# Three passes for all K-tiles of gate and up, and the low parts of the down weights all on GpSimd

## The chip, the cores and the metric

The kernel runs on one core of a Trainium2 chip. The metric is the device time of one execution, in microseconds. The engines are TensorE (PE in the profile; PEld is its weight load), VectorE (DVE), ScalarE (ACT), GpSimd (POOL) and SyncE (SP), which issues most DMAs.

## The reference

Two layers work on 512 tokens of width 1024, all in float32. Each layer is a mixer (three kinds of attention, gates, output projection) and then a mixture of 16 experts:

```python
h = rms_norm(x, norm_mix_g[l]);  x = x + hybrid_mixer(h, ...)
h = rms_norm(x, norm_ffn_g[l]);  x = x + hier_moe(h, ...)
# hier_moe: every token picks one group of four, and two experts in it
hid = silu(h @ w_g[e]) * (h @ w_u[e])     # w_g, w_u: 1024 x 256 for each expert
hid = hid * gate[e]                       # 0 for tokens that did not pick e
y   = sum over e of hid @ w_d[e]          # w_d: 256 x 1024
```

## The kernel before

A float32 matrix product is made in one of two ways. Native: one matmul on the float32 operands, which the trace shows as two records. Three passes (`three`, L895 to L897): each operand is split into a high part in the type fp32r and a low part, the difference, and three matmuls add high times low, low times high and high times high.

The mixer's dense products are all in three passes: GpSimd makes the high part (L763) and the low part (L769) of the streamed weights. After the mixer the rows are normalized, the router picks, and every expert gets up to 128 tokens, whose rows GpSimd gathers from DRAM (L807). A last loop takes experts with more tokens (one such block in this input).

The experts are counted from 0 in the order of work. For each of them TensorE makes, in this order: gate and up together (`gate_up`, eight K-tiles of 128x512, gate in the left half), the transposes of the next expert's gathered rows (`turn_gathered`, L1152), the down product of the expert before (`down`, two halves c of 512 columns) and the two transposes of its own hidden rows (`turn_hidden`, L1210). Experts 0 and 1 are native in gate and up. From 2 to 15, K-tiles 0 to 3 are native (L1200) and K-tiles 4 to 7 are in three passes. The down product is in three passes but for expert 15.

The other engines' orders in step e of the expert loop are written out by hand:

- ScalarE: silu(e); the first half of the transposed rows of e+1, four copies with the norm's gain as scale (L1565), and the high part of the second half (L1576); the result rows of e-1, first half (L1602); the high parts of the down weights of e, two of 1024 columns (`weights_hi`, L1593, each waits until the down product of e-1 has used its half); the high parts of K-tiles 4 to 7 of e+2 with the gain as scale (`gate_up_hi`, L1583).
- VectorE: hidden product of e (L2206); low part of the second half of the rows of e+1 (L2171); result rows of e-1, second half (L2216); high and low part of the hidden rows (L2226, L2228); the low part of half c = 1 of the down weights (`down_lo_half`, L2192); the low parts of K-tiles 4 to 7 of e+2, 512 columns each (`gate_up_lo`, L2184). Steps 0 to 3 also hold small operations of the routing.
- GpSimd: the gather for e+3 (L807); the low part of half c = 0 of the down weights, two subtractions of 512 columns (`weights_lo`, L831); the scattered addition of the result rows of e-1 to the residual in DRAM (L821).

TensorE's `gate_up(e)` waits for VectorE's and ScalarE's parts of the rows of e, and each three-pass K-tile for its low part.

The weights of an expert come in three pieces of 1 MB: K-tiles 0 to 3 of gate and up, K-tiles 4 to 7, and down. They pass through a ring of six slots in `work`, in the order `PIECE_ORDER`, issued by SyncE (L686 to L693), each after a wait for the slot's last user. Gate and up rows are 1 KB long in DRAM, and each goes to its own partition; down rows are 4 KB long.

## Time and profile before

| | us |
|---|---|
| median of 3 runs | 1399.3 (1398.26 to 1400.98) |
| the profiled execution | 1398.75 |
| its span, first to last instruction | 1396.8 |
| TensorE busy | 1363.1 (98%) |
| VectorE busy | 863.2 (62%) |
| GpSimd busy | 728.4 (52%) |
| ScalarE busy | 585.8 (42%) |

The expert stage of the first layer lies from about 520 to 690 us, that of the second from about 1209 to the end. The rest is the mixer. Matmuls overlap in the pipeline, so that the time from one start to the next is what one costs, not its duration. In a timeline neighbours of one kind are merged into one row with their count.

### The profile page before, as it was taken

What the parts mean: (1) busy time and instruction counts of PE and PEld (TensorE: products, weight loads), DVE (VectorE), ACT (ScalarE), POOL (GpSimd) and SP (SyncE); (2) the same over time, 40 slices, a digit from 0 to 9 for tenths busy, and PEclk for the clock granted to TensorE, in tenths of its full rate; (3) what the DMA queues carried; (4) which work ended last, traced back from release to release, by engine and by line L of the source; (5) the groups of instructions that cost most, each with busy time, mean ns of one, the idle gap of its engine ahead of it and who ended that gap; (6) DMA issues with size and microseconds to landing.
All of it is one profiled execution on the core that took longest, in us unless ns stands there. A gap on an engine that the chain in (4) does not pass through costs nothing.

```text
span 1396.8 us, 19901 instructions
## 1 busy us (share of the span) xinstructions
PE 1363.1 (98%) x6916; PEld 1036.2 (74%) x6916; DVE 863.2 (62%) x2057; ACT 585.8 (42%) x1334; POOL 728.4 (52%) x587
## 2 busy tenths in 40 slices
PE   7999999999999999999889999999999999999997
PEld 5788877777777876767477888777777778667674
DVE  4487866656684347776346787666567741576772
ACT  4323333343433135676443432433434421466761
POOL 4566645445345634566555576454444455255663
PEclk9999999999999999999889999999999999999999
DMA  5436422222212659999732242222222128599995
GB/s 154 130 100 172 121 83 73 73 74 97 90 61 76 232 217 318 340 360 350 190 118 76 61 135 81 75 76 74 89 80 90 61 88 292 213 330 350 346 348 130
DMA packets 148570, 224.28 MB, mean 161 GB/s; under 512 B 18635, under 2 KB 95877, under 8 KB 148463
## 3 DMA queue, kind: packets, MB, share of 16 engines
q1 hardware_dynamic: 136030, 197.59, 43.6%
q0 software_dynamic: 9936, 16.81, 5.1%
q10 hardware_dynamic: 2496, 8.52, 1.6%
q8 instruction: 59, 0.97, 0.3%
q14 instruction: 49, 0.39, 0.1%
HBM read 215.47 MB, written 31.25 MB: 177 GB/s over the span
## 4 chain that ended last, share of the span: by engine, by line
PE 92%; DVE 4%; ACT 1%; POOL 1%; DMA 1%; issue 1%; SPq 0%; POOLq 0%; ACTq 0%; DVEq 0%
PE bank L895 22%; PE bank L897 21%; PE bank L896 21%; PE bank L1200 9%; PE bank L1071 4%; PE bank L1083 3%; PE bank L1104 2%; PE bank L1152 2%; PE bank L1024 1%; PE bank L1094 1%; DVE probs L1913 1%; PE bank L1037 1%; POOL w_lo L769 1%; PE bank L1162 1%; PE bank L1360 0%
## 5 line engine op out<-in xcount | busy, mean ns | idle before, releaser
L769 POOL TENSOR_TENSOR w_lo<-raw,w_hi 128x512 fp32r<-128x512 f32 (+2 forms) x288 | 359.2, 1268 | 16.4 <-ACT w_hi L1641 4.6
L763 POOL TENSOR_SCALAR w_hi<-raw 128x1024 fp32r<-128x1024 f32 (+2 forms) x142 | 149.4, 1052 | 417.3 <-PE bank L897 414.5
L896 PE MATMUL bank<-w_hi,hT_lo 128*128 128x512 f32 (+2 forms) x696 | 258.8, 372 | 0.0
L895 PE MATMUL bank<-w_lo,hT_hi 128*128 128x512 f32 (+2 forms) x576 | 216.8, 376 | 2.1 <-DVE hT_lo L1738 1.2
L897 PE MATMUL bank<-w_hi,hT_hi 128*128 128x512 f32 (+2 forms) x576 | 211.8, 368 | 0.0
L895 PE MATMUL bank<-hT_lo,w_hi 128*128 128x512 f32 x384 | 159.5, 415 | 0.0
L897 PE MATMUL bank<-hT_hi,w_hi 128*128 128x512 f32 x384 | 150.7, 393 | 0.0
L896 PE MATMUL bank<-hT_hi,w_lo 128*128 128x512 f32 x384 | 150.2, 391 | 0.0
L896 PEld LDWEIGHTS bank<-w_hi,hT_lo 128*128 128x128 f32 x696 | 131.6, 189 | 20.3
L1200 PE MATMUL bank<-work,ptmp 128*128 128x512 f32 x288 | 129.4, 593 | 1.0 <-ACT ptmp L1565 1.0
L895 PEld LDWEIGHTS bank<-w_lo,hT_hi 128*128 128x128 f32 x576 | 108.7, 189 | 28.0 <-issue 8.7
L831 POOL TENSOR_TENSOR w_lo<-work,w_hi 128x512 fp32r<-128x512 f32 x64 | 105.7, 1672 | 43.8 <-ACT w_hi L1593 43.8
L897 PEld LDWEIGHTS bank<-w_hi,hT_hi 128*128 128x128 f32 x576 | 108.7, 189 | 17.9
L895 PEld LDWEIGHTS bank<-hT_lo,w_hi 128*128 128x128 f32 x384 | 72.1, 188 | 32.8 <-issue 20.5
L1200 PEld LDWEIGHTS bank<-work,ptmp 128*128 128x128 f32 x288 | 52.0, 190 | 54.0 <-issue 52.6
L807 POOL DMA_INDIRECT probs<-normed_dram,slot_token x32 | 33.3, 1040 | 102.5 <-PE bank L1152 80.4
L897 PEld LDWEIGHTS bank<-hT_hi,w_hi 128*128 128x128 f32 x384 | 72.1, 188 | 16.5
L896 PEld LDWEIGHTS bank<-hT_hi,w_lo 128*128 128x128 f32 x384 | 72.3, 188 | 12.5
L895 PE MATMUL bank<-oT_lo,w_hi 128*128 128x512 f32 x192 | 79.4, 413 | 0.5 <-DVE hT_lo L1971 0.5
L897 PE MATMUL bank<-oT_hi,w_hi 128*128 128x512 f32 x192 | 76.0, 396 | 0.0
L896 PE MATMUL bank<-oT_hi,w_lo 128*128 128x512 f32 x192 | 75.7, 394 | 0.0
L1496 ACT ACTIVATE probs<-probs,job_neg 128x256 f32<-128x256 f32 (+5 forms) x128 | 66.5, 523 | 15.4 <-DVE job_neg L1896 15.4
(331 smaller groups left out, 2651.4 us busy)
## 6 DMA issues: line engine op xcount, KB each, us to landing
work<-in_w_ff_gate SPq DMA_DIRECT2D x66, 512.0 KB
work<-in_w_ff_up SPq DMA_DIRECT2D x66, 512.0 KB
work<-in_w_ff_down SPq DMA_DIRECT2D x33, 1024.0 KB
raw<-in_w_gate SPq DMA_DIRECT2D x48, 512.0 KB, 3.8
raw<-in_w_in SPq DMA_DIRECT2D x40, 512.0 KB, 3.6
raw<-in_w_branch SPq DMA_DIRECT2D x24, 512.0 KB, 3.6
raw<-in_w_out SPq DMA_DIRECT2D x16, 512.0 KB, 3.9
normed_dram<-mixed ACTq DMA_DIRECT2D x8, 512.0 KB, 2.7
```

Source lines behind the costliest of these rows:

```text
L763: nc.gpsimd.tensor_scalar(w_hi[:, two, :, 0:w], raw[:, slot, :, 0:w], 1.0, 0.0, ALU.mult, ALU.add).then_inc(split_hi, 1)
L769: last = nc.gpsimd.tensor_tensor(w_lo[:, two, kk, 0:w], raw[:, slot, kk, 0:w], w_hi[:, two, kk, 0:w].bitcast(F32), ALU.subtract)
L807: nc.gpsimd.indirect_dma_start(out=gather_rows[:, e % 2, :], out_offset=None, in_=xn_dram, in_offset=bass.IndirectOffsetOnAxis(ap=rows, ax ...
L831: last = nc.gpsimd.tensor_tensor(w_lo[:, c, f, :], rows[:, f, c * 512:(c + 1) * 512], w_hi[:, c, f, :].bitcast(F32), ALU.subtract)
L895: nc.tensor.matmul(out_ap, s_hi, m_lo, start=start, stop=False)
L896: nc.tensor.matmul(out_ap, s_lo, m_hi, start=False, stop=False)
L897: return nc.tensor.matmul(out_ap, s_hi, m_hi, start=False, stop=stop)
L1071: last = nc.tensor.matmul(S[m][:, cols], q[r, job.u, job.i * P:(job.i + 1) * P], k[r, keys], start=True, stop=True)
L1083: last = nc.tensor.transpose(T[0][:, col:col + P], prob_bufs[job.g % 3][:, mm, b * P:(b + 1) * P], ident[:, :])
L1104: last = nc.tensor.matmul(O[HD * m:HD * (m + 1), job.i * P:(job.i + 1) * P], v, p[:, m, b * P:(b + 1) * P], start=(b == 0), stop=(b == len ...
L1200: last = nc.tensor.matmul(G[e % 2][:, :], et[:, e % 2, kt * P:(kt + 1) * P], gate_up_piece(n % RING)[:, :, kk, :], start=(kt == 0), stop=( ...
L1496: last = nc.scalar.activation(p, p, ACT.Exp, bias=job_neg[:, g % 4, m:m + 1], scale=-1.0, accum_out=job_sum[:, g % 4, m:m + 1])
```

## The change

All eight K-tiles of gate and up of experts 2 to 15 go through three passes (`SPLIT_FROM = 0`). ScalarE makes their high parts in four operations of two K-tiles (1024 columns), VectorE their low parts likewise, four of 1024 columns, which are written over the raw weights in their slot; so the slot is free only when TensorE has used it. VectorE also makes the low part of the first half of the gathered rows. VectorE's half of the down weights' low parts moves to GpSimd, which makes all four subtractions of 512 columns, over the raw weights too.

The ring gets nine slots, three for each kind of piece: six in `work`, two in `X`, one in the buffer `w_lo`. The order of loads changes, and the pieces of expert 2 no longer wait for expert 0. Gate and up rows are moved two at a time, in runs of 2 KB, so that a partition holds neighbouring rows; the columns of the normalized rows are put in the same order.

The norm's gain is no longer a scale of ScalarE's and VectorE's copies: GpSimd multiplies it into the rows ahead of the routing, eight operations of 512 columns, seven of them before it takes the inverse root and one after; ScalarE then scales these rows by the root. Copies of transposed rows are single operations without scale.

```diff
-RING = 6
+SLOTS_OF_PART = ((0, 3, 6), (1, 4, 7), (2, 5, 8))
+AHEAD = 3
+
+ROW_RUN = 2
...
-FIRST_SPLIT = 2
-
-PIECE_ORDER = [(2, 0), (2, 1), (2, 2), (3, 0), (3, 1), (4, 1)]
-for before in range(2, N_EXPERTS - 1):
-    PIECE_ORDER += [(e, part) for e, part in ((before + 2, 0), (before + 1, 2), (before + 3, 1)) if e < N_EXPERTS]
...
+FIRST_SPLIT, SPLIT_FROM = 2, 0
+SPLIT_PAIRS = (8 - SPLIT_FROM) // 2
+
+PIECE_ORDER = [(2, 2), (2, 0), (2, 1), (3, 0), (3, 1)]
+for e in range(4, N_EXPERTS):
+    PIECE_ORDER += [(e, 0), (e, 1), (e - 1, 2)]
+PIECE_ORDER.append((N_EXPERTS - 1, 2))
...
                 def load_piece(e, part):
-                    n = PIECES * e + part
-                    slot, old = n % RING, e - 2
+                    old = e - AHEAD
                     if old >= 0 and part == 0:
                         sp.wait_ge(first_half, old + 1)
-                    elif old >= 0 and part == 1 and splits(old):
-                        sp.wait_ge(gu_lo, split_count(old))
                     elif old >= 0 and part == 1:
                         sp.wait_ge(gu_done, old + 1)
                     elif old >= 0:
-                        sp.wait_ge(down_lo, old + 2)
-                        if old:
-                            sp.wait_ge(down_lo_dve, old)
+                        sp.wait_ge(down_done, 2 * (old + 1))
...
+                def gain_step(t, c):
+                    pool.wait_ge(g_free, 4 * (OUT_CHUNK + c) + t + 1)
+                    cols = slice(c * 512, (c + 1) * 512)
+                    in_order = lambda rows: rows.rearrange("p (a n k) -> p a k n", n=P, k=ROW_RUN)
+                    nc.gpsimd.tensor_tensor(xn[:, t, cols].rearrange("p (a k n) -> p a k n", n=P, k=ROW_RUN),
+                                            in_order(X[:, t, cols]), in_order(ffn_gain[:, cols]),
+                                            ALU.mult).then_inc(x_gained, 1)
+
+                pool.wait_ge(gain_in, 32)
+                for t in range(TT):
+                    gain_step(t, 0)
+                for t in range(TT - 1):
+                    gain_step(t, 1)
                 pool.wait_ge(ms_done, TT + 1)
                 pow_step(row_rs[:, 1, :], row_ms[:, 1, :], TT).then_inc(rs_done, 1)
+                gain_step(TT - 1, 1)
...
                 def weights_lo(e):
                     rows = down_rows(e)
-                    for c in range(1 if e else 2):
+                    for c in range(2):
                         pool.wait_ge(down_hi, 2 * e + c + 1)
                         for f in range(2):
-                            last = nc.gpsimd.tensor_tensor(w_lo[:, c, f, :], rows[:, f, c * 512:(c + 1) * 512],
+                            last = nc.gpsimd.tensor_tensor(down_low(e)[:, f, c * 512:(c + 1) * 512],
+                                                           rows[:, f, c * 512:(c + 1) * 512],
                                                            w_hi[:, c, f, :].bitcast(F32), ALU.subtract)
                         last.then_inc(down_lo, 1)
...
+                        if kt == SPLIT_FROM:
+                            pe.wait_ge(et_dve, e + 1)
+                        if (kt - SPLIT_FROM) % 2 == 0:
+                            pe.wait_ge(gu_lo, split_pairs(e - 1) + pair + 1)
+                        last = three(G[e % 2][:, :], et_hi[:, e % 2, rows], et_lo[:, e % 2, rows],
+                                     pair_hi_of(e, kt)[:, (kt - SPLIT_FROM) % 2, :], gate_up_low(e, part)[:, :, kk, :],
+                                     kt == 0, kt == KT - 1)
...
             def gate_up_hi(e):
 
-                n = PIECES * e + 1
-                act.wait_ge(piece_in[n % RING], 32 * (n // RING + 1))
-                for kk in range(4):
-                    nc.scalar.activation(gu_hi_bufs[e % 2][kk].rearrange("p (h n) -> p h n", h=2),
-                                         gate_up_piece(n % RING)[:, :, kk, :], ACT.Copy,
-                                         scale=pcol[:, ROW_FFN + 4 + kk:ROW_FFN + 5 + kk]).then_inc(gu_hi, 1)
+                for part, kk, kt in split_tiles():
+                    if kt == SPLIT_FROM or kk == 0:
+                        act.wait_ge(arrived(e, part), loaded(e, part))
+                    nc.scalar.activation(pair_hi_of(e, kt).rearrange("p k (h n) -> p k h n", h=2),
+                                         gate_up_piece(e, part)[:, :, kk:kk + 2, :].rearrange("p h k n -> p k h n"),
+                                         ACT.Copy).then_inc(gu_hi, 1)
...
             def gate_up_lo(e):
 
-                n = PIECES * e + 1
-                for kk in range(4):
-                    v.wait_ge(gu_hi, split_count(e - 1) + kk + 1)
-                    nc.vector.scalar_tensor_tensor(gu_lo_bufs[e % 2][kk].rearrange("p (h n) -> p h n", h=2),
-                                                   gate_up_piece(n % RING)[:, :, kk, :], pcol[:, ROW_FFN + 4 + kk:ROW_FFN + 5 + kk],
-                                                   gu_hi_bufs[e % 2][kk].bitcast(F32).rearrange("p (h n) -> p h n", h=2),
-                                                   ALU.mult, ALU.subtract).then_inc(gu_lo, 1)
-
-            def down_lo_half(e):
-
-                v.wait_ge(down_hi, 2 * e + 2)
-                nc.vector.tensor_tensor(w_lo[:, 1, :, :], down_rows(e)[:, :, 512:1024], w_hi[:, 1, :, :].bitcast(F32),
-                                        ALU.subtract).then_inc(down_lo_dve, 1)
+                for n, (part, kk, kt) in enumerate(split_tiles()):
+                    v.wait_ge(gu_hi, split_pairs(e - 1) + n + 1)
+                    nc.vector.tensor_tensor(gate_up_low(e, part)[:, :, kk:kk + 2, :].rearrange("p h k n -> p k h n"),
+                                            gate_up_piece(e, part)[:, :, kk:kk + 2, :].rearrange("p h k n -> p k h n"),
+                                            pair_hi_of(e, kt).bitcast(F32).rearrange("p k (h n) -> p k h n", h=2),
+                                            ALU.subtract).then_inc(gu_lo, 1)
```

## Rows read from the trace of the kernel before

**Rows 1.** The page: busy time and the chain that ended last; TensorE's native group.

```profile
PE 1363.1 (98%) x6916; PEld 1036.2 (74%) x6916; DVE 863.2 (62%) x2057; ACT 585.8 (42%) x1334; POOL 728.4 (52%) x587
...
PE 92%; DVE 4%; ACT 1%; POOL 1%; DMA 1%; issue 1%; SPq 0%; POOLq 0%; ACTq 0%; DVEq 0%
...
L1200 PE MATMUL bank<-work,ptmp 128*128 128x512 f32 x288 | 129.4, 593 | 1.0 <-ACT ptmp L1565 1.0
```

**Rows 2.** Timeline of TensorE: start us, us, engine, line, what, count.

```profile
542.07 1.45 PE L1200 MATMUL bank<-work,ptmp 128*128 128x512 f32 x3
...
604.21 3.60 PE L1200 MATMUL bank<-work,ptmp 128*128 128x512 f32 x8
...
608.34 0.40 PE L895 MATMUL bank<-oT_lo,hT_hi 128*128 128x512 f32 x1
...
610.44 1.04 PE L1152 MATMUL bank<-ident,probs 128*128 128x128 f32 x8
...
614.28 3.60 PE L1200 MATMUL bank<-work,ptmp 128*128 128x512 f32 x8
...
674.66 2.74 PE L1200 MATMUL bank<-work,ptmp 128*128 128x512 f32 x6
```

**Rows 3.** Timeline of VectorE in the same period (in brackets: idle before it, releaser).

```profile
600.98 0.42 DVE L2206 TENSOR_TENSOR sq<-sq,bank 128x256 f32<-128x256 f32 x1 [0.46 <-ACT sq L1685]
602.76 0.69 DVE L2171 TENSOR_TENSOR hT_hi<-bank,hT_hi 128x512 fp32r<-128x512 f32 x1 [1.36 <-ACT hT_hi L1576]
604.19 0.75 DVE L2216 TENSOR_SCALAR mixed<-bank,slot_weight 128x512 f32<-128x512 f32 x1 [0.74 <-PE bank L897]
...
605.65 1.25 DVE L2192 TENSOR_TENSOR w_lo<-work,w_hi 128x1024 fp32r<-128x1024 f32 x1
606.83 1.76 DVE L2184 SCALAR_TENSOR_TENSOR hT_hi<-work,pcol,hT_lo 128x512 fp32r<-128x512 f32 x1
```

**Rows 4.** Timeline of ScalarE in the same period.

```profile
601.00 1.14 ACT L1565 ACTIVATE ptmp<-bank,pcol 128x128 f32<-128x128 f32 x4
602.02 0.62 ACT L1576 ACTIVATE hT_hi<-bank 128x512 fp32r<-128x512 f32 x1
...
603.42 1.99 ACT L1593 ACTIVATE w_hi<-work 128x1024 fp32r<-128x1024 f32 x2
605.31 2.55 ACT L1583 ACTIVATE hT_lo<-work,pcol 128x512 fp32r<-128x512 f32 x4
```

**Rows 5.** Timeline of GpSimd in the same period.

```profile
602.17 1.03 POOL L807 DMA_INDIRECT probs<-normed_dram,slot_token  x1 [2.17 <-PE bank L1152]
604.55 3.49 POOL L831 TENSOR_TENSOR w_lo<-work,w_hi 128x512 fp32r<-128x512 f32 x2 [1.34 <-ACT w_hi L1593]
...
605.79 2.25 POOL L831 TENSOR_TENSOR w_lo<-work,w_hi 128x512 fp32r<-128x512 f32 x1
...
608.20 1.86 POOL L821 DMA_INDIRECT residual_dram<-mixed,slot_token  x1 [0.15 <-issue]
```

**Rows 6.** Windows: busy us (instructions) of each engine, PEclk, DMA share, GB/s.

```profile
549.00:569.00 20.00, 20.00 (x86) 13.93 (x85) 17.70 (x34) 14.02 (x26) 12.80 (x8) 1.00 1.03 340
...
599.00:649.00 50.00, 50.00 (x210) 34.91 (x209) 37.03 (x51) 35.22 (x65) 31.62 (x21) 1.00 1.06 354
...
606.00:608.00 2.00, 2.00 (x7) 1.00 (x6) 2.00 (x2) 1.86 (x4) 2.00 (x1) 1.00 1.03 409
```

**Rows 7.** Timeline of VectorE in the first experts.

```profile
544.66 1.24 DVE L2128 TENSOR_SCALAR raw<-rank 128x8 f32<-128x8 f32 x1
...
547.32 1.42 DVE L2184 SCALAR_TENSOR_TENSOR hT_hi<-work,pcol,hT_lo 128x512 fp32r<-128x512 f32 x2
```

**Rows 8.** Timelines of GpSimd and VectorE ahead of the routing.

```profile
493.59 1.29 POOL L769 TENSOR_TENSOR w_lo<-raw,w_hi 128x512 fp32r<-128x512 f32 x1
...
504.92 1.02 POOL L751 TENSOR_TENSOR row_rs<-row_ms,half_neg 128x4 f32<-128x4 f32 x1 [10.04 <-DVE row_ms L1773]
...
509.04 0.24 DVE L2016 TENSOR_TENSOR score<-bank,row_rs 128x80 f32<-128x80 f32 x1 [0.71 <-PE bank L1282]
```

**Rows 9.** DMA in the stretch from 549 to 665 us.

```profile
DMA packets 29117, 40.39 MB, mean 348 GB/s; under 512 B 2681, under 2 KB 24807, under 8 KB 29110
...
q1 hardware_dynamic: 25806, 34.19, 84.5%
```

229 lines of the change are left out of this document (129 added, 100 removed).

## The prediction

> **What bounds the kernel now.** I read the page first, busy shares and the chain that ended last [rows 1]. TensorE is busy 98% of the span and holds 92% of the chain. Every microsecond that the expert stage takes from TensorE shortens the kernel, as long as the other engines keep pace. So the question is who comes next when TensorE gets shorter.
>
> Then one period of the expert stage on TensorE [rows 2]. Expert 8's native K-tiles begin at 604.21 us and expert 9's at 614.28 (experts are counted from 0, as in the code): a period of 10.07 us. Four native K-tiles are eight records in 3.60 us, the last of them 0.59 long [rows 1]: (3.60 - 0.59)/7 = 0.43 us from one to the next, 0.86 for a K-tile. Of the three-pass matmuls nine lie between 608.34 and the transposes at 610.44, 0.233 us each, so 0.70 for a K-tile. The part outside gate/up (transposes, down product, turning of the hidden rows) runs from 610.44 to 614.28: 3.84 us.
>
> Then the same period on the other three engines [rows 3 to 5], and the stage by windows [rows 6]. VectorE is busy 7.4 of 10 us (8.85 in the experts that also carry routing work), ScalarE 7.0, GpSimd 6.3, DMA more than full at about 350 GB/s.
>
> What decides is inside [rows 3, 5]. GpSimd's low part of 128x512 takes 1.27 to 1.29 us alone [rows 5, 8] (3.49 for two, of which the second starts 1.24 after the first), and 2.25 when it is issued at 605.79, behind VectorE's subtraction of 605.65 to 606.90: it ends 1.14 us after that one. VectorE's next operation of 512 columns, 0.74 where nothing interferes (two in 1.42 [rows 7]), takes 1.76: it ends 0.55 us after GpSimd's. Even an operation on eight columns took 1.24 us beside such a pair [rows 7]. Operations of VectorE that read two operands from SBUF and GpSimd's subtractions take turns. Those with one operand in a bank (0.69 to 0.75 us) show no such stretch.
>
> **The change, part by part.**
>
> *TensorE.* Four K-tiles go from 0.86 to 0.70 us. With the first three-pass matmul after a native one, which comes later by 0.4 than its fellows, the trace has 6.23 us for the eight (604.21 to 610.44) and the change 24 x 0.233 = 5.58: 0.65 us less per expert, in 14 experts and two layers 18.2 us less. A TensorE-bound period would be 24 x 0.233 + 3.84 = 9.42 us.
>
> *ScalarE.* The four copies of 1.14 us with a scale become one copy of 0.62; four high parts of 512 columns (2.55) become four of 1024, by [rows 4] 0.97 apart, 3.9. It would end them 8.9 us after gate/up ended: still inside 9.42. Not the limit.
>
> *VectorE.* Per expert one more low part of the gathered rows (0.61 apart), and the low parts of the weights, 1.18 + 4 x 0.66 us before, become four of 1024 columns at 1.18, the step from 605.65 to the next operation: 4.72 [rows 3]. Unhindered, from the end of one expert's low parts to the start of the next ones: hidden product 0.40, two low parts of gathered rows 1.22 (durations of 0.42 and 0.69 less the overlap with the next), then from the row at 604.19 to the one at 605.65 (result rows, hidden rows high and low) 1.46, together 3.08. With 4.72 that is 7.80.
>
> *GpSimd.* Four subtractions per expert for two. It starts them when ScalarE's first high part of the down weights is there, at 604.55, or 4.18 us after gate/up ended (one period before 610.44, at 600.37).
>
> *The two together.* VectorE runs: 3.08 us, then its four, in turn with what GpSimd still has. In turn, GpSimd's costs 1.14 (above) and VectorE's of 1024 columns 0.55 x 2 = 1.10. Let T be the period and count from the end of VectorE's low parts. TensorE's next gate/up waits for the low parts of its rows, 1.72 us, takes 5.58 and so ended at 7.30 - T for this expert; GpSimd starts at 11.48 - T. Two of its four (2.45 us) are through when VectorE gets to its own. VectorE waits w = 11.48 - T + 2.45 - 3.08 = 10.85 - T for the second, then 1.10 + 1.14 + 1.10 + 1.14 + 1.10 + 1.18 = 6.76. T = 3.08 + w + 6.76 = 20.69 - T, so T = 10.35, and w = 0.5. VectorE with GpSimd's turns in between becomes the bound, 0.28 us above today's 10.07 and 0.93 above TensorE's 9.42.
>
> GpSimd just fits: gather 1.03, scatter 1.86, 0.5 of gaps, and 6.9 from the first to the last low part, 10.3.
>
> *Over a layer.* From expert 2's gate/up to expert 15's are 13 periods. Before, 12 of 10.07 and one of 11.78 with a small product in it: 132.6. After, 13 x 10.35 = 134.6, plus the routing operations that VectorE has in the first experts and that TensorE covers now: the windows with them show 8.85 us busy for 7.4, 1.45 in two experts, and about 2 from 544.7 to 547.3 in the one before, GpSimd's turn among them, between the low part that leaves and the next [rows 6, 7]; I take 3.5 in all, since the later experts catch up part of it. That is 138.1, 5.5 more; expert 15's own gate/up gives 0.65 back. 4.85 a layer, 9.7 in both.
>
> *The head of the expert stage.* GpSimd gets eight multiplications by the gain. It is idle from 494.9 to 504.9, before the inverse root [rows 8]. Seven at 1.27 fill 8.9 us of those 10; nothing is late. They have strided operands that no row shows: from 1.27 up to twice that, the root comes up to 8 us later; 3 us of that are free (VectorE reads the root at 509.04), so 0 to 5 a layer. I take 0.5, since 1.27 is a row of the same operation. The longer wait of the first copy in expert 1 (1.14 to 0.62) gives 0.5 back. Three more slots let the pieces of expert 2 load while the routing runs, beside the normalized rows that the first gather waits for. I count that as nothing, and as up to 1 us a layer in the range, if those rows come later.
>
> *DMA.* Gate and up rows are moved in runs of 2 KB for 1 KB, the same bytes. In the busy stage (549 to 665 us) 40.39 MB go in 116 us, 348 GB/s [rows 9]; with 34.19 MB of weights in it at 3.15 MB an expert, that is 10.67 us an expert, already longer than 10.07; the lead of the early loads is used up in the course of a layer. No row shows runs of 2 KB in this stage; they lie between today's 348 GB/s and the 409 of the best two microseconds [rows 6], where down pieces with their longer runs pass: 10.7 us, or 2.1 MB less dear by 0.9, 9.8. With one expert's pieces earlier and ten microseconds of slack in the ring of nine, this doesn't bind at 10.35; it would at 9.42, late in each layer.
>
> The profiled execution took 1398.75 us, 1.95 more than its span, 0.55 below the median of 1399.3. 1399.3 + 9.7 = **1409 us**.
>
> **The rivals.**
>
> *Taking turns costs little* (15%). If VectorE's and GpSimd's operations mix more finely, VectorE's 7.80 us fit into 9.42, and TensorE stays the bound: 1399.3 - 18.2 = 1381. For it: the arithmetic of VectorE alone. Against: 2.25 for 1.27 and 1.76 for 0.74. It decides at 0.8 us of turns per expert: unhindered, VectorE begins when ScalarE's first high part is there, 6.05 us after gate/up ended (4.94 to the start of that group in [rows 4], 1.05 for one of 1024 columns), and ends 4.72 later, 1.35 into the next period; TensorE starts to wait when it is 2.15 into it. The turns counted above are 2.8 us.
>
> *DMA or half the waiting* (10%). The period falls between 9.8 and 10.0, and what the early experts lose to routing eats most of it: 13 x 9.9 + 3.5 - 132.6 = -0.4 a layer: 1396 to 1400, no change.
>
> *GpSimd's own loop closes* (15%). If it starts so late that VectorE gets in after its first, all four alternate: 1.24 + 3 x 2.24 = 7.96, with 3.37 of gather, scatter and gaps 11.3 us. That state holds itself once entered, since GpSimd then always starts late. From expert 8 on it gives 7 x 0.95 = 6.7 more a layer, 13.4 in both: 1423. The same price results if an operation keeps the other out for its whole length, 1.27 and 1.25: T is 10.8 and 2 x 13 x 0.45 = 12 are added, 1421. The Trainium skill, SBUF — State Buffer, Who interferes with whom, has the second: whoever issues second blocks until the first finishes. The rows lie a little below it (1.14 for 1.27, 1.10 for 1.25).
>
> The Trainium skill, GPSIMD Engine Reference, Engine selection, advises against elementwise work of two inputs on GpSimd, about twice as slow as VectorE. Here 1.27 for 512 columns stands against 1.25 for 1024. By the rule the down half belongs on VectorE; that would cost VectorE 1.18 and spare it two turns of 1.14.
>
> **Chances.** Forecast 60% (its own range 1402 to 1416), turns cheap 15%, near zero 10%, GpSimd's loop or full exclusion 15%. The range takes the near-zero case, the closed loop and part of the cheap one: 1384 to 1424. A measurement of this kernel can tell about 0.2%, 2.8 us, from no change. Slower by more: 0.68; within: 0.10; faster: 0.22.
>
> **What the changed profile would show.** Right: TensorE's gate/up group starts after a wait of some 0.9 us for VectorE's low part of the gathered rows; periods of 10.1 to 10.6; GpSimd's low parts at a mean near 1.75 us with a spread from 1.27 to 2.3, VectorE's of 1024 columns from 1.25 to 2.3; both busy over 9 of 10 us. Three-pass K-tiles at 0.70. Wrong: gate/up back to back at 9.4 (turns cheap); waits of ScalarE for DMA pieces (DMA); waits for GpSimd ahead of the down product, and periods of 11.3 (closed loop); a gap ahead of the routing with GpSimd's multiplications in it (strides).

## The result and the profile after

The changed kernel takes **1448.2 us** (1447.34 to 1448.59), the kernel before 1399.6 in the same session: a ratio of 1.0347 (95% interval 1.0334 to 1.036), 48.6 us slower. The forecast was 1409, with 1384 to 1424 as its range. The direction was right, the size five times too small. The two spans differ by 1446.7 - 1396.8 = 49.9 us.

The page of the changed kernel (busy time, the chain that ended last, GpSimd's low parts of the down weights), against [rows 1]:

```profile
PE 1363.8 (94%) x7028; PEld 1062.8 (73%) x7028; DVE 956.1 (66%) x2057; ACT 604.1 (42%) x1238; POOL 842.7 (58%) x659
...
PE 75%; DVE 13%; issue 5%; ACT 3%; DMA 3%; POOL 1%; ACTq 0%; SPq 0%; POOLq 0%; DVEq 0%
...
L915 POOL TENSOR_TENSOR work_low<-work,w_hi 128x512 fp32r<-128x512 f32 x80 | 116.4, 1486 | 10.1 <-ACT w_hi L1675 9.8
```

VectorE now holds 13% of the chain, and DMA and "issue" have 3% and 5% where they had 1% each. TensorE's busy time has not fallen, though its K-tiles got cheaper: some of its matmuls ran at the low clock (the mean granted clock is 0.982, before 0.993).

To find the place I took the start of the transposes of the next expert's rows (L1152 before, L1237 after), which stand at the end of each gate/up. Their distances are the periods. Differences of layer 1 are given behind those of layer 0:

| | before, us | after, us | after less before, layer 0 / 1 |
|---|---|---|---|
| head: up to the end of expert 0's gate/up | 527.6 | 532.3 | +4.7 / +6.9 |
| experts 0 to 2, two periods | 10.55, 10.16 | 10.65, 9.44 | -0.6 / -0.7 |
| expert 2 to 3 | 10.06 | 15.32 | +5.3 / +4.1 |
| expert 3 to 4 | 10.07 | 9.42 | -0.7 / -0.6 |
| expert 4 to 5 | 10.06 | 21.12 | +11.1 / +10.4 |
| expert 5 to 6 | 11.81 | 11.14 | -0.7 / -0.7 |
| experts 6 to 14, mean of eight | 10.06 | 10.62 | +4.5 / +4.5 |
| expert 14 to 15 | 12.99 | 14.09 | +1.1 / +1.1 |

The sum is 24.7 and 25.0 us. Three things stand out: the head, two single periods, and the steady ones.

**The steady periods.** The changed kernel's timelines of VectorE (first) and GpSimd (second) from 647 us on, to be read against [rows 3, 5] (the first two rows of GpSimd overlap, the third of its four subtractions stands in both):

```profile
647.47 4.04 DVE L2268 TENSOR_TENSOR X_low<-X,hT_lo 128x1024 fp32r<-128x1024 f32 x2 [0.66 <-ACT hT_lo L1666]
...
669.00 2.27 DVE L2268 TENSOR_TENSOR work_low<-work,hT_lo 128x1024 fp32r<-128x1024 f32 x1
...
673.43 2.35 DVE L2268 TENSOR_TENSOR work_low<-work,hT_hi 128x1024 fp32r<-128x1024 f32 x2
...
689.86 6.09 DVE L2268 TENSOR_TENSOR work_low<-work,hT_lo 128x1024 fp32r<-128x1024 f32 x2
```

```profile
666.41 3.79 POOL L915 TENSOR_TENSOR w_lo<-w_lo_raw,w_hi 128x512 fp32r<-128x512 f32 x3 [0.53 <-ACT w_hi L1675]
668.89 3.54 POOL L915 TENSOR_TENSOR w_lo<-w_lo_raw,w_hi 128x512 fp32r<-128x512 f32 x2
...
688.66 5.06 POOL L915 TENSOR_TENSOR work_low<-work,w_hi 128x512 fp32r<-128x512 f32 x4
```

At 669.00 the turns are those that the prediction counted: VectorE's 1024 columns take 2.27 us beside GpSimd and 1.17 (two in 2.35) alone. Two experts later it is different. GpSimd's four subtractions run back to back, 5.06 us, and VectorE's two take 6.09, so the first of them 4.95: it waited for the whole rest of the chain. I call such an operation caught. The periods come in threes, 9.7, 11.1 and 11.2 us: the first has two turns, the second three turns (2.8 us) behind a wait of 0.66 us for ScalarE's high parts (the row at 647.47), the third a catch. TensorE pays with waits for the low parts of the gathered rows, as forecast (602 to 665 us; total, times, longest):

```profile
PE bank L980 <- DVE ptmp_low L2261: 2.9, 3, 1.0
```

**The period of 21.1 us**, expert 4 to 5. The changed kernel's timelines of VectorE, GpSimd and TensorE, and two windows (columns as in [rows 6]), in this order:

```profile
581.88 0.20 DVE L2228 TENSOR_TENSOR raw<-raw 128x32 f32<-128x32 f32 x1
582.11 0.19 DVE L2230 TENSOR_TENSOR raw<-raw 128x32 f32<-128x32 f32 x1
582.22 5.68 DVE L2228 TENSOR_TENSOR raw<-raw 128x32 f32<-128x32 f32 x1
587.94 0.19 DVE L2230 TENSOR_TENSOR raw<-raw 128x32 f32<-128x32 f32 x1
588.05 0.41 DVE L2284 TENSOR_TENSOR sq<-sq,bank 128x256 f32<-128x256 f32 x1
```

```profile
581.82 1.08 POOL L891 DMA_INDIRECT probs<-normed_dram,slot_token  x1 [0.30 <-issue]
582.92 2.50 POOL L915 TENSOR_TENSOR work_low<-work,w_hi 128x512 fp32r<-128x512 f32 x2
...
591.18 2.53 POOL L905 DMA_INDIRECT residual_dram<-mixed,slot_token  x1 [3.33 <-DVE mixed L2294]
```

```profile
588.51 0.69 PE L1296 MATMUL bank<-ident,sq 128*128 128x128 f32 x2 [7.58 <-DVE sq L2284]
589.92 0.76 PE L980 MATMUL bank<-X_low,hT_hi 128*128 128x512 f32 x1 [0.71 <-DVE ptmp_low L2261]
...
598.28 1.03 PE L1237 MATMUL bank<-ident,probs 128*128 128x128 f32 x8
```

```profile
582.00:589.00 7.00, 0.48 (x2) 0.29 (x2) 6.93 (x7) 3.98 (x5) 5.83 (x5) 0.76 0.77 228
589.00:594.00 5.00, 4.29 (x11) 3.24 (x11) 4.96 (x8) 0.00 (x0) 2.53 (x1) 0.50 0.01 3
```

A routing operation on 32 columns, 0.20 us in its two neighbours, takes 5.68. It was issued 0.70 us before GpSimd's first subtraction, and ends with the fourth (at 587.84). VectorE's hidden product stands behind it in order, TensorE idles for 7.58 us, and then its granted clock is 0.50, the level of 1.2 GHz: gate/up of expert 5 takes 598.28 - 589.92 = 8.36 us where 5.58 were forecast. The period from expert 2 to 3 is a smaller copy: three operations on eight columns of 1.22 us each beside GpSimd's chain, and a gate/up of 8.20 us (559.54 to 567.74), its first 5 us at the low clock.

**The head.** GpSimd's first gather waits for the last store of normalized rows. In layer 1 that store was issued at 1225.89 us and the gather began at 1235.94 (timelines of ScalarE's queue and of GpSimd):

```profile
1225.89 0.33 ACTq L1759 DMA_DIRECT2D normed_dram<-mixed  x1
```

```profile
1235.94 1.13 POOL L891 DMA_INDIRECT probs<-normed_dram,slot_token  x1 [14.51 <-DMA normed_dram<-mixed]
```

That is 10.1 us for 4.7 before (1200.79 to 1205.49), with expert 2's pieces under way (issued from 1216.91 to 1223.9). The view of the DMA issues has it too: from issue to landing the median of these stores is 8.1 us, 2.7 before.

```profile
normed_dram<-mixed ACTq DMA_DIRECT2D x8, 512.0 KB, 8.1
```

TensorE waits 4.70 us for the gathered rows there and 2.6 in layer 0. Ahead of it VectorE's last sum of squares (503.81 in layer 0) took 2.10 us for 0.69 beside GpSimd's seventh multiplication by the gain, which makes the inverse root 1.5 us late [rows 8]. The seven multiplications themselves took 10.45 us, 1.5 each, and ended at 505.37, 0.45 behind the start of the root before the change. GpSimd's timeline:

```profile
494.92 10.45 POOL L869 TENSOR_TENSOR mixed<-X,probs 128x512 f32<-128x512 f32 x7
```

### The profile page after: what moved, and what is told of

It reads as the page before. It is cut to its first block, busy times and chain, and to the rows that moved or that the text cites. A ratio compares the mean times of both kernels' runs of the same rounds, so it can differ in the third digit from the quotient of the medians.

```text
span 1446.7 us, 20111 instructions
## 1 busy us (share of the span) xinstructions
PE 1363.8 (94%) x7028; PEld 1062.8 (73%) x7028; DVE 956.1 (66%) x2057; ACT 604.1 (42%) x1238; POOL 842.7 (58%) x659
## 4 chain that ended last, share of the span: by engine, by line
PE 75%; DVE 13%; issue 5%; ACT 3%; DMA 3%; POOL 1%; ACTq 0%; SPq 0%; POOLq 0%; DVEq 0%
PE bank L980 20%; PE bank L982 19%; PE bank L981 19%; PE bank L1156 4%; DVE X_low L2268 3%; PE bank L1168 3%; PE bank L1189 2%; DVE work_low L2268 2%; PE bank L1277 1%; PE bank L1109 1%; PE bank L1179 1%; DMA normed_dram<-mixed 1%; ACT w_hi L1675 1%; DVE probs L1994 1%; PE bank L1237 1%
## 5 line engine op out<-in xcount | busy, mean ns | idle before, releaser
L915 POOL TENSOR_TENSOR work_low<-work,w_hi 128x512 fp32r<-128x512 f32 x80 | 116.4, 1486 | 10.1 <-ACT w_hi L1675 9.8
L980 PEld LDWEIGHTS bank<-hT_lo,w_hi 128*128 128x128 f32 x384 | 72.1, 188 | 32.9 <-issue 20.5
L891 POOL DMA_INDIRECT probs<-normed_dram,slot_token x32 | 38.2, 1194 | 80.2 <-PE bank L1237 45.6
L982 PEld LDWEIGHTS bank<-hT_hi,w_hi 128*128 128x128 f32 x384 | 72.1, 188 | 16.5
L915 POOL TENSOR_TENSOR w_lo<-w_lo_raw,w_hi 128x512 fp32r<-128x512 f32 x40 | 62.1, 1578 | 9.8 <-ACT w_hi L1675 9.8
L980 PE MATMUL bank<-work_low,hT_hi 128*128 128x512 f32 x144 | 59.6, 414 | 8.3 <-DVE ptmp_low L2261 7.6
```

Source lines behind the costliest of these rows:

```text
L891: nc.gpsimd.indirect_dma_start(out=gather_rows[:, e % 2, :], out_offset=None, in_=xn_dram, in_offset=bass.IndirectOffsetOnAxis(ap=rows, ax ...
L915: last = nc.gpsimd.tensor_tensor(down_low(e)[:, f, c * 512:(c + 1) * 512], rows[:, f, c * 512:(c + 1) * 512], w_hi[:, c, f, :].bitcast(F32 ...
L980: nc.tensor.matmul(out_ap, s_hi, m_lo, start=start, stop=False)
L982: return nc.tensor.matmul(out_ap, s_hi, m_hi, start=False, stop=stop)
```

## The experiments

Each is an edit of the changed kernel. Times are medians, beside 1448.2 for the changed kernel and 1399.6 (1399.1 to 1400.2 in the sessions) for the one before.

### The head: loads behind the stores

```diff
+                sp.wait_ge(xn_out, 16 * TT)
                 for e, part in PIECE_ORDER:
```

> The changed kernel, but SyncE issues the three early loads of expert 2 only after the normalized rows are in DRAM. My theory: in the changed kernel the last store of these rows is issued at 513.34 us and GpSimd's first gather, which waits for it, starts at 522.50, 9.2 us later; in layer 1 it is 1225.89 and 1235.94, 10.1 us, against 1200.79 and 1205.49, 4.7 us, before the change. The early loads are in the way. Without them TensorE's waits of 2.6 us (layer 0) and 4.70 us (layer 1) for the gathered rows vanish, and the low clock behind the second (0.79 from 1240 to 1248 us) with it: 1448.2 - 2.6 - 4.7 - 1.5 = 1439 us. Rival: the pieces of expert 2 are then late themselves, ScalarE's high parts of expert 2 wait, and the time goes back to where it was, 1446 to 1449. Second rival: the head is late because the inverse root comes 1.5 us later in either layer, and the stores matter little: 1446.

**1443.2 us**, ratio to before 1.0303 (1.0283 to 1.0323). Half of what was expected. Layer 1's head fell by 3.2 us (from the end of one layer's last gate/up to the end of the next one's first: 539.7 to 536.5), layer 0's by 0.8. The gather started at 517.98 for 522.50, but now expert 2's loads (issued 515.8 to 518.4) ran beside the gather itself: its rows reached TensorE at 525.8. I had taken away one collision and made another.

### The head: loads behind the gathers

```diff
+                for i in range(2):
+                    sp.wait_ge(gathered[l][i], 16)
                 for e, part in PIECE_ORDER:
```

> The changed kernel, but SyncE issues the early loads of expert 2 only when GpSimd's first two gathers have landed. With the loads after the stores alone (the run before this one) the gather started at 517.98 us instead of 522.50, but its rows reached TensorE at 525.8, 7.8 us later, where 5.3 had been enough before the change: the loads stood in the gather's way instead. My theory: now neither is hindered, TensorE's waits of 2.6 and 4.70 us and the low clock behind the second (about 1.5 us) go, and the head is late by the inverse root's 1.5 us alone: 1448.2 - 8.8 = 1439.4 us. Rival: the pieces of expert 2, issued at about 523 us, are now late for ScalarE, and gate/up of expert 2 starts later by as much: 1443 to 1448.

**1438.3 us**, ratio 1.0276 (1.0259 to 1.0293). As expected: TensorE goes from the native K-tiles to the gathered rows without a wait, and the head of layer 1 is 533.5 us against 532.8 before the change. The two heads are 3.7 and 6.2 us shorter than in the changed kernel, 9.9 of the 11.6 us lost there. Its timeline of TensorE in layer 0:

```profile
521.24 1.88 PE L1279 MATMUL bank<-work,ptmp 128*128 128x512 f32 x4
522.96 0.60 PE L1256 MATMUL bank<-ident,probs 128*128 128x128 f32 x4
```

One execution, the profiled one, took 1427.6. In its layer 1 the routing operation slipped through at 1283.64, 0.42 us into GpSimd's gather, before the subtractions; in layer 0 the same operation was caught, and the period was 20.5 us again. Timelines of VectorE and GpSimd in layer 1:

```profile
1283.64 0.18 DVE L2230 TENSOR_TENSOR raw<-raw 128x32 f32<-128x32 f32 x1
```

```profile
1283.22 1.10 POOL L893 DMA_INDIRECT probs<-normed_dram,slot_token  x1 [0.30 <-issue]
```

The periods there are 12.6, 11.0 and 11.2 us for 14.2, 9.45 and 20.5, 9.3 us less in the three. That a race so close falls differently in each execution would explain the spread from 1427.6 to 1439.2; only one execution has a trace.

### The head: and fewer multiplications ahead of the root

```diff
-                for t in range(TT - 1):
-                    gain_step(t, 1)
+                gain_step(0, 1)
                 pool.wait_ge(ms_done, TT + 1)
                 pow_step(row_rs[:, 1, :], row_ms[:, 1, :], TT).then_inc(rs_done, 1)
-                gain_step(TT - 1, 1)
+                for t in range(1, TT):
+                    gain_step(t, 1)
```

> As the run with the gathers first, and GpSimd makes five of its eight multiplications by the gain ahead of the inverse root and three behind it, instead of seven and one. In the changed kernel VectorE's last sum of squares took 2.10 us instead of 0.69 beside the seventh of them, and the root came 1.5 us later (506.4 for 504.92). My theory: the root is on time again, ScalarE's scaling waits for no multiplication by more than 0.2 us: 1.5 us less in each layer than the run with the gathers first, 3 in both, 1436.4 us. Rival: ScalarE waits for the multiplications moved behind the root (1.5 us each, three of them), so that nothing is won: as the other run, or up to 2 us above.

**1433.6 us**, ratio 1.0243 (1.0206 to 1.0279), but its four executions lie at 1430.0, 1430.1, 1437.1 and 1439.3, perhaps the two outcomes of the race above (in the traced one, 1437.1, the operation is caught in both layers), so 3 us can't be read from the median. The trace shows the step itself: the sum of squares takes 0.69 us again and the root starts at 504.97 for 504.92 before. It brought less than the 1.5 us a layer that was expected: layer 1's head is 532.7, as before the change and 0.8 less than in the run before this one, but in layer 0 the first gather starts at 517.56 for 517.65, and the head is no shorter. VectorE's timeline in this run:

```profile
503.79 0.69 DVE L1851 CUSTOM_DVE_ANT_0 ptmp<-X 128x512 f32<-128x512 f32 x1
```

### GpSimd held back in step 4

```diff
                 def weights_lo(e):
                     rows = down_rows(e)
+                    if e == 4:
+                        pool.wait_ge(e_hot, 1)
```

> The changed kernel, but in step 4 GpSimd starts its four low parts of the down weights of expert 4 only after VectorE's last small routing operation of step 3. In the changed kernel this operation (128x32) is issued at 582.22 us, before GpSimd's first subtraction at 582.92, and ends at 587.90 with the fourth of them; expert 5's gate/up then starts at about 590 and takes 8.5 us at a granted clock of 0.50 and 0.81 instead of 5.6. My theory: the two engines don't take turns here; an operation that loses at the boundary of GpSimd's chain waits for the whole chain. Held back, the operation is through by 583.2, gate/up of expert 5 ends near 591 instead of 598.3, and the layer gains 7 us, both 14: 1434 us. Rival (TensorE's clock is low for reasons of its own, and the period is long by that): at most the 3 us of waiting that one low part takes, 1442 to 1448. Rival (the operation waits for something of VectorE's own): no change, 1448. Rival (GpSimd's chain merely moves onto the low parts of expert 6's weights): half of the gain, 1441.

**1435.3 us**, ratio 1.0243 (1.022 to 1.0265): 12.9 us less, for next to no waiting on GpSimd. The same operation takes 0.18 us, and GpSimd's chain begins 1.11 us after the gather's start, where it was 1.10 (timelines of VectorE and GpSimd):

```profile
582.68 0.18 DVE L2230 TENSOR_TENSOR raw<-raw 128x32 f32<-128x32 f32 x1
```

```profile
582.27 1.08 POOL L891 DMA_INDIRECT probs<-normed_dram,slot_token  x1 [0.31 <-issue]
583.38 4.99 POOL L917 TENSOR_TENSOR work_low<-work,w_hi 128x512 fp32r<-128x512 f32 x4
```

The period is 14.4 and 14.2 us for 21.1 and 20.5. The gather alone doesn't hold VectorE out; the subtractions behind it do.

### A gap in GpSimd's chain

The gather for the third expert ahead is moved between the low parts of c = 0 and of c = 1.

```diff
                     for c in range(2):
+                        if c and 1 <= e <= N_EXPERTS - 3:
+                            gather_tokens(e + 3)
                         pool.wait_ge(down_hi, 2 * e + c + 1)
...
-                    if e + 3 <= N_EXPERTS:
+                    if e == 0:
                         gather_tokens(e + 3)
```

> The changed kernel, but GpSimd makes the gather for the third expert ahead (about 1.0 us and 0.3 before it) between the low parts of half c = 0 and c = 1 of the down weights instead of ahead of both: two chains of two subtractions for one of four. In the changed kernel four back to back held a VectorE operation for 4.95 us in every third steady period and for 5.7 in step 4. My theory: a caught operation waits until GpSimd's subtractions have a gap; with a gap after two none takes over 2.5 + 1.3 us, the period of 21.1 falls to 14 or less, and the steady mean from 10.62 to some 10.4: 1448 - 2 x (7 + 2) = 1430 us. Rival (the gather holds VectorE out as well, or an operation is caught for a fixed number of turns): unchanged, 1445 to 1450. Rival: c = 1 comes 1.3 us later and the down product waits: over 1450.

**1454.4 us**, ratio 1.0399 (1.0382 to 1.0416). The time was forecast wrongly, of the mechanism only the first part came true. This run's timelines of VectorE and GpSimd in step 4:

```profile
583.57 3.96 DVE L2226 TENSOR_SCALAR raw<-o_rows,raw 128x128 f32<-128x128 f32 x2
587.46 0.18 DVE L2230 TENSOR_TENSOR raw<-raw 128x32 f32<-128x32 f32 x1
587.67 0.19 DVE L2232 TENSOR_TENSOR raw<-raw 128x32 f32<-128x32 f32 x1
587.78 3.24 DVE L2230 TENSOR_TENSOR raw<-raw 128x32 f32<-128x32 f32 x1
```

```profile
584.21 3.04 POOL L917 TENSOR_TENSOR work_low<-work,w_hi 128x512 fp32r<-128x512 f32 x2
587.41 1.05 POOL L891 DMA_INDIRECT probs<-normed_dram,slot_token  x1 [0.16 <-issue]
588.49 2.47 POOL L917 TENSOR_TENSOR work_low<-work,w_hi 128x512 fp32r<-128x512 f32 x2
```

The caught operation, a TENSOR_SCALAR this time, comes free at the gap, 587.3, behind two subtractions and not four. Then the same operation as ever is caught by the second pair. Two catches of 3.8 and 3.2 us cost what one of 5.7 did: the period is 21.3. There are new catches at 551.0 and 563.5 us too, of 3.3 and 3.1 us, and the period from expert 2 to 3 is longer, 16.6 us for 15.3 (layer 1: 16.7 for 14.2). The rival with over 1450 named the time, but its wait is small here: from 545 to 700 us TensorE waits for GpSimd's low parts twice, 0.8 us in all. In the steady part no VectorE operation above 2.4 us is left, but from expert 8 on every period is 10.6 to 10.9, and the mean of the eight 10.66 for 10.62: what a catch costs once, turns cost spread out. So the catches of the steady part are not shown to cost more than turns would.

### Matmuls in the waiting time

Matmuls whose result is thrown away, first ahead of gate/up of experts 3 and 5 (12 and 28 of them), then ahead of the transposes of the hidden rows of experts 2 and 4 (8 and 30):

```diff
-                        if kt == SPLIT_FROM:
-                            pe.wait_ge(et_dve, e + 1)
                         if (kt - SPLIT_FROM) % 2 == 0:
                             pe.wait_ge(gu_lo, split_pairs(e - 1) + pair + 1)
+                        if kt == SPLIT_FROM:
+                            for _ in range({3: 12, 5: 28}.get(e, 0)):
+                                nc.tensor.matmul(G[e % 2][:, :], pair_hi_of(e, kt)[:, 0, 0:P],
+                                                 pair_hi_of(e, kt)[:, 0, :], start=True, stop=True)
+                            pe.wait_ge(et_dve, e + 1)
```

```diff
+                    if e in (2, 4):
+                        pe.wait_ge(hid_done, e)
+                        pe.wait_ge(gu_lo, split_pairs(e) + 1)
+                        for _ in range({2: 8, 4: 30}[e]):
+                            nc.tensor.matmul(G[(e + 1) % 2][:, :], pair_hi_of(e + 1, 0)[:, 0, 0:P],
+                                             pair_hi_of(e + 1, 0)[:, 0, :], start=True, stop=True)
                     if e < N_EXPERTS:
                         turn_hidden(e)
```

> The changed kernel with matmuls whose result is thrown away (12 of 128x512 ahead of gate/up of expert 3, 28 ahead of that of expert 5), made while TensorE waits for the gathered rows' low parts. In the changed kernel TensorE sat idle for 7.6 us ahead of expert 5 and 1.95 and 0.85 ahead of expert 3, the granted clock then was 0.50 for 5 us (1.2 GHz), and gate/up took 8.36 and 8.2 us instead of 5.58. My theory: the long periods are half waiting and half the clock; with TensorE busy the clock stays at 1.0, each gate/up takes 5.6, and the layer gains 5.4 us, both 10.8: 1437.4 us. Rival (the clock is low for another reason): 1448, or above it if the matmuls delay the next gate/up.

> As the run with matmuls whose result is thrown away, but 8 of them ahead of the transposes of expert 2's hidden rows and 30 ahead of those of expert 4. In the run before this one they came too late: TensorE works in order and sat idle for 7.6 us at these transposes, not at gate/up, so the matmuls ran behind the idle time, at 0.52 of the clock, and only added to the period (25.6 us for 21.1), though gate/up of expert 3 and 5 behind them did take 5.6 us. My theory: made in the idle time itself, they keep the clock up and cost nothing: up to 5.4 us less in a layer than the changed kernel, 10.8 in both, 1437.4 us, and periods near 12.7 and 18.3 instead of 15.3 and 21.1. Rival (the clock falls in spite of the matmuls): 1448 or more.

**1458.8 us** (ratio 1.043, 1.0413 to 1.0448) and **1437.5 us** (1.0273, 1.0258 to 1.0288). The first missed: TensorE's idle time lay at the transposes, so the matmuls ran behind it. The second is the forecast to 0.1 us, but by luck, as its timelines of TensorE, VectorE and GpSimd and a window show:

```profile
579.47 6.97 PE L1424 MATMUL bank<-hT_lo 128*128 128x512 f32 x30
586.27 0.38 PE L1296 MATMUL bank<-ident,sq 128*128 128x128 f32 x2
...
591.97 0.71 PE L1237 MATMUL bank<-ident,probs 128*128 128x128 f32 x5
```

```profile
579.32 0.18 DVE L2234 TENSOR_TENSOR raw<-raw 128x32 f32<-128x32 f32 x1
...
586.69 0.42 DVE L2310 CAST hT_lo<-bank 128x256 fp32r<-128x256 f32 x1 [4.77 <-PE bank L1296]
```

```profile
580.03 5.06 POOL L915 TENSOR_TENSOR work_low<-work,w_hi 128x512 fp32r<-128x512 f32 x4
```

```profile
586.00:592.00 6.00, 6.00 (x29) 4.85 (x29) 5.28 (x6) 0.00 (x0) 0.85 (x1) 1.00 0.60 120
```

Gate/up of expert 5 takes 5.6 us at a granted clock of 1.00. But the routing operation is not caught in this execution (0.18 us, in layer 1 too), though nothing holds GpSimd back. The 30 matmuls, 6.97 us, took the place of the idle time, and now VectorE waits 4.77 us for TensorE. So the run changed two things, and its 10.7 us are not the price of the clock.

That price is better read from the changed kernel: gate/up of experts 3 and 5 took 8.20 and 8.36 us in layer 0, 7.09 and 7.72 in layer 1, for 5.6 at full clock: 9.0 us in all. The first of the two runs agrees. Its routing operation is caught as ever (5.69 us), and behind the matmuls gate/up of expert 5 takes 5.4 us (597.97 to 603.41).

### Four K-tiles, the rest of the change kept

```diff
-FIRST_SPLIT, SPLIT_FROM = 2, 0
+FIRST_SPLIT, SPLIT_FROM = 2, 4
```

> The changed kernel with only K-tiles 4 to 7 of experts 2 to 15 in three passes, as before the change; ring, loads, gain on GpSimd and all four down low parts on GpSimd stay. VectorE then has two low parts of 1024 columns instead of four and one low part of gathered rows instead of two: 7.80 - 2.36 - 0.61 = 4.83 us and at most two or three turns of 1.1, below TensorE's 10.07. My theory: the expert stage costs what it cost before (TensorE's 10.07 a period), and only the loss at the head stays, 4.7 in layer 0 and 6.9 in layer 1: 1399.6 + 11.6 = 1411 us, up to 4 us more if the small routing operations are still caught behind GpSimd's four. Rival (all of the loss comes with the four K-tiles): 1400. Rival (the new ring and its loads, or GpSimd's own loop with four low parts, hold the stage up): over 1425.

**1412.8 us**, ratio 1.0089 (1.0069 to 1.0109), for 1411. The periods are those before the change to 0.05 us: 10.06 in the steady part, 10.04 from expert 2 to 3 and from 4 to 5. The ring, the runs of 2 KB and GpSimd's four subtractions cost nothing in the stage; 13.8 us lie at the heads (6.4 and 7.5). VectorE's operations are caught here too, six of them for 4.3 us, but VectorE has the time (timeline of this run; the second of the two takes 1.2 us):

```profile
622.70 5.45 DVE L2268 TENSOR_TENSOR work_low<-work,oT_hi 128x1024 fp32r<-128x1024 f32 x2 [0.65 <-ACT oT_hi L1666]
```

### The down half back on VectorE

```diff
+            def down_lo_half(e):
+                v.wait_ge(down_hi, 2 * e + 2)
+                nc.vector.tensor_tensor(down_low(e)[:, :, 512:1024], down_rows(e)[:, :, 512:1024],
+                                        w_hi[:, 1, :, :].bitcast(F32), ALU.subtract).then_inc(down_lo_dve, 1)
...
-                    for c in range(2):
+                    for c in range(1 if e else 2):
                         pool.wait_ge(down_hi, 2 * e + c + 1)
```

> The changed kernel, but the low part of half c = 1 of the down weights is VectorE's again, one operation of 1024 columns, in experts 1 to 14; GpSimd has two subtractions instead of four. By the working of the prediction: VectorE has 3.08 + 5 x 1.18 = 8.98 us, waits some 0.9 us for GpSimd's second, and then meets no more turns: a period of 9.9 instead of the 10.62 measured, 10 steady periods of two layers each gaining 0.7, 14 us; and in step 4 the routing operation is caught behind two subtractions instead of four, 2.5 us earlier, with less time at the low clock, 8 us in both layers: 1448.2 - 22 = 1426 us. Rival (VectorE's sum decides and turns don't): the period rises to 11 and more, 1455. Rival (a gain only from step 4): 1440.

**1411.2 us**, ratio 1.0083 (1.0065 to 1.0101), 15 us better than forecast. The steady periods are some 9.4 and 10.3 in turn, mean 9.82 (9.9 forecast). The rest is the first experts: 11.7, 10.3 and 10.9 us in layer 0 for 15.3, 9.4 and 21.1, since only one small operation meets GpSimd's chain in step 2 (1.26 us), and those of step 3 are over before the next chain begins (578.12 and 578.79); and 12.4 for 14.1 at the end. VectorE is busy more, 59.1 of 60 us for 57.2, and the kernel is faster by 37 us (window of this run):

```profile
602.00:662.00 60.00, 58.12 (x282) 47.58 (x281) 59.10 (x67) 48.13 (x62) 42.99 (x26) 1.00 1.04 370
```

### No down low parts on GpSimd

```diff
-                        for f in range(2):
-                            last = nc.gpsimd.tensor_tensor(down_low(e)[:, f, c * 512:(c + 1) * 512],
-                                                           rows[:, f, c * 512:(c + 1) * 512],
-                                                           w_hi[:, c, f, :].bitcast(F32), ALU.subtract)
-                        last.then_inc(down_lo, 1)
+                        pool.sem_inc(down_lo, 1)
...
-                                     down_low(e)[:, f, c * 512:(c + 1) * 512], f == 0, f == 1)
+                                     w_hi[:, c, f, :], f == 0, f == 1)
```

> The changed kernel, but GpSimd leaves out all low parts of the down weights (it only signals), and TensorE's down product multiplies by the high parts in their place, with as many matmuls; the output lacks that part. My theory: VectorE without turns has 7.80 us a period and TensorE becomes the bound at 9.42; the routing operations are not caught. From expert 1 to expert 15 the stage then lasts what it did before the change less 13 x 0.65 us, 145.6 - 8.5 = 137 us instead of 165.5 in layer 0 and 174.3 in layer 1; the loss at the head stays: 1399.6 + 11.6 - 18.2 = 1393 us. Rival (VectorE's own load, or the DMA at 3.15 MB an expert, holds the stage up too): periods of 9.8 to 10.1 even without GpSimd's subtractions, 1400 to 1408, growing later in a layer if it is the DMA.

**1393.7 us**, ratio 0.9959 (0.9948 to 0.9969), for 1393. The periods are 9.31 and 9.42 nearly throughout (10.3 from expert 3 to 4, and 9.74 once among the last), with DMA at 371 GB/s (window of this run):

```profile
602.00:662.00 60.00, 60.00 (x299) 49.78 (x298) 49.05 (x64) 49.40 (x65) 16.32 (x13) 1.00 1.05 371
```

From expert 1 on the stage is 16.5 us shorter than before the change in the two layers, so TensorE's 18 us are nearly all there, and neither VectorE's own load nor the DMA is much in their way. The 54 us between this run and the changed kernel come from GpSimd's subtractions by way of VectorE: in the changed kernel's expert stage TensorE waits for none of the low parts that GpSimd makes.

### Head and hold together

The two edits at the head and the wait in step 4.

> The changed kernel with both changes at the head (early loads behind the first two gathers, three multiplications by the gain behind the root) and with GpSimd held back in step 4 until the last small routing operation. If the parts add: the pair at the head gave 1448.2 - 1433.6 = 14.6, of which about 4 by runs without the long catch, so 10 to 11; the hold gave 12.9: 1448.2 - 23.4 = 1425 us. What is left above the kernel before, 25 us, is then the cost of four subtractions a period beside VectorE's low parts: eight steady periods at 10.6 for 10.06 (9 us in both layers), expert 3's and 5's periods of 14.2 (16 us). Rival (they overlap: what one removes the other had removed): 1433 or more.

**1421.8 us**, ratio 1.0171 (1.0154 to 1.0188). The parts add up: 14.6 + 12.9 = 27.5 by the medians (the expectation took 23.4), 26.4 measured.

### Versions meant to beat both

All three have the two edits at the head and the down half on VectorE. The first has `SPLIT_FROM = 2`, six K-tiles in three passes. The second has all eight and the routing operations moved:

```diff
                     if e < N_EXPERTS - 1:
                         et_out(e + 1)
+                    if e == 1:
+                        route_rows()
+                    if e in (2, 3):
+                        route_blocks(e - 2)
...
-                    if e == 1:
-                        route_rows()
                     if splits(e + 2):
                         gate_up_lo(e + 2)
-                    if e in (2, 3):
-                        route_blocks(e - 2)
```

The third has both.

> A version meant to beat both: K-tiles 2 to 7 of experts 2 to 15 in three passes, the low part of half c = 1 of the down weights on VectorE, the early loads behind the first two gathers, three of GpSimd's multiplications by the gain behind the inverse root. My theory: TensorE's period is 10.07 - 2 x 0.16 = 9.75 us; VectorE has 3.08 + 1.18 + 3 x 1.18 = 7.80 us and at most one or two turns of 1.1 with GpSimd's two subtractions, so TensorE stays the bound; the head is as before the change: 1399.6 - 2 x 13 x 0.32 = 1391.3 us, and up to 5 more if the small routing operations are caught behind GpSimd. Rival (turns bind here too): periods of 10 and more, 1400 to 1405.

> All eight K-tiles in three passes, the low part of half c = 1 of the down weights on VectorE, early loads behind the gathers, three multiplications by the gain behind the root, and VectorE's small routing operations of steps 1 to 3 moved ahead of its result rows, before GpSimd's subtractions of that step begin. My theory: the steady periods are those of the run with the down half on VectorE, 9.31 and 10.33 in turn, 9.83 in the mean; experts 3 to 5 take 9.5 instead of 11.7, 10.3 and 10.9 since nothing is caught: about 4.5 us less in a layer than before the change, 1399.6 - 9 = 1390.6 us. Rival: the moved operations make the result rows and the hidden rows late, TensorE waits for these, and nothing is won over leaving them: 1396 to 1400. Rival: the catch moves to another operation: over 1400.

> K-tiles 2 to 7 in three passes, with the down half on VectorE, both changes at the head, and the routing operations moved as in the run above. My theory: as the run with six K-tiles without what the routing costs it there, 1391.3 us or 1 us less, since expert 3 to 5 then keep to 9.75 us as well. Rival (the moved operations delay the result rows): 1 to 4 us above the run with six K-tiles.

**1392.6 us** (ratio 0.9953, 0.9938 to 0.9968), **1400.9 us** (1.0007, 0.9998 to 1.0016) and **1391.1 us** (0.9941, 0.9928 to 0.9954). With six K-tiles every period from expert 2 on is TensorE's: 9.67 and 9.75 (11.5 and 12.6 where more work stands in one), with no wait for VectorE, which has 8 us of 60 free (window of the third):

```profile
602.00:662.00 60.00, 60.00 (x272) 45.43 (x271) 51.88 (x63) 43.52 (x63) 42.52 (x25) 1.00 1.02 357
```

With eight the second missed by 10 us. The steady periods are as expected, but from expert 3 to 4 stand 12.3 and 13.8 us: from 556 to 572 us VectorE is busy 15.8 of 16 and TensorE 13.6, at a clock of 1.00. VectorE is the bound there, and the routing's 1.5 us only moved within it. The third is the fastest of all, 8.3 us below the kernel before; what it has over the first, 1.5 us, is about the width of their spreads.

## Why the prediction was wrong

It forecast +9.7 us and measured +48.6; its own steps, with both layers together:

- *TensorE's saving of 18.2 us.* Right. Three-pass K-tiles cost 0.23 us a matmul, TensorE-bound periods are 9.42, and 16.5 us of the saving are there when GpSimd's low parts are gone. Six tiles get about half of it (8.3 us) with nothing in the way.
- *ScalarE, the DMA, GpSimd's own loop, the ring.* Right for all but ScalarE: none binds, and the rivals on DMA and on GpSimd's loop fell. ScalarE's high parts keep VectorE waiting for 0.66 us in one period of three, which the sum had at nothing.
- *Turns in the steady part, T = 10.35.* The price of a turn was right (1.27 and 2.27, 1.17 and 2.27 us), the term mis-sized: 10.62. Eight periods of 0.27 in two layers are 4.3 us. The period forecast, with 2.8 us of turns, is one of three, and it is 11.1 long and not 10.35, with the wait for ScalarE in it; in another there are only two turns, 9.7; in the third "in turn, GpSimd's costs 1.14 and VectorE's 1.10" failed, and VectorE's first operation was held for 3.7 us (4.95 for 1.21). None of the eight lies between the 10.1 and 10.6 that were forecast. What the catch adds to the 0.27 is open: the run with the gather in between has none in the steady part, and a mean of 10.66.
- *"3.5 in all" for the routing operations.* This is the step that failed worst. The first five periods took 66.4 and 64.7 us for 5 x 10.35 + 3.5 = 55.3 forecast: 20.6 us. I gave each small operation at most a turn (1.24 us in [rows 7]) and took VectorE's waiting for TensorE's. One operation waited for four subtractions, and after TensorE's wait the clock fell. The hold gave back 12.9 us; the slow gate/ups of experts 3 and 5 are 9.0 us of the loss, in part of the same loss. With no catch the sum held: in layer 1 of the run with the gathers first, where no operation is caught in these five periods and the clock stays up, they take 55.5 us.
- *The head, "I count that as nothing".* 11.6 us, of which the loads behind the gathers gave back 9.9. The early loads of expert 2, "up to 1 us", held the stores and the first gather up: 2.6 and 4.7 us of waiting for rows, and the low clock after the second (0.79 from 1240 to 1248 us). "0.5 for the multiplications" was short too: seven took 10.45 us for 8.9, and VectorE's last sum of squares, which reads X twice from SBUF, stood beside them, so the root came 1.5 us late in each layer. With the root in time again little was won (0.8 us in layer 1), so what this cost is not shown.
- *The last period.* Forecast 0.65 shorter, it was 1.1 longer, 3.5 us in both layers; with half of the chain it was 12.4 for 14.1, so this too belongs to GpSimd's four.

The four gaps, 4.3 + 20.6 + 11.6 + 3.5 = 40.0, are the difference between 9.7 and the 49.7 us of the table.

The rival with full exclusion (1421) described the lock better than the forecast did, and was still 27 us short: no case in my list had the clock in it. The Trainium skill, SBUF — State Buffer, Who interferes with whom, says that whoever issues first holds the pair of SBUF ports that VectorE and GpSimd share for a whole instruction while the other blocks. The turns agree (2.27 for 1.17); the waits of 4.95 and 5.68 us go beyond it, since they last over three and four instructions of GpSimd. The Trainium skill, GPSIMD Engine Reference, Engine selection, sends elementwise work of two inputs to VectorE. The traces agree: one half moved back made the kernel 37 us faster, though VectorE was busier for it in the steady part (59.1 of 60 us for 57.2).

What is not settled: why an operation is caught at one moment and not at another. The three caught in the steady part of layer 0 (625.73, 657.76, 689.86) were issued 1.19 to 1.20 us after the chain began, just ahead of its second subtraction; the one at 669.00, 2.59 us after, took turns. With four K-tiles they were issued 0.5 us into the second subtraction. The routing operations caught were issued 0.37 to 0.42 us into the gather ahead of the chain, but three at 0.40 to 0.42 got through with nothing holding GpSimd (1283.64 above, and both layers of the run with matmuls before the hidden rows). In these three the period from expert 2 to 3 had been short, 12.6 or 12.7 us, and 14.0 or more where the operation was caught; why that should matter is open. That GpSimd's next instruction claims the memory while the gather still runs would fit the catches, but no run isolates it.

## What to carry to other kernels

Work of two SBUF operands on GpSimd is priced at what it does to VectorE's next operation on SBUF, up to the length of the whole uninterrupted chain, and not per turn. All operations caught here have no operand in a bank; most read two tensors, but with the gather in between a TENSOR_SCALAR was held too. Where VectorE has time to spare, a catch costs nothing, as with four K-tiles. So look for the smallest VectorE operation of that kind that stands ahead of something TensorE needs, and order it before the chain with a semaphore: one wait was worth 12.9 us. Price a stall of TensorE at its length plus the slow matmuls behind it. And where loads may start earlier than before, ask which small transfer on the critical path they will meet: the stores first, then the gather.
